# One stage for the first block's input: layer loads, latent rows, MLA attention, with 30 half-tile projections between its steps

## What is computed

```
proj = h @ w_in                                  # 1024 -> 448 + 1920 columns
c_q, c_kv, k_pe, rw = split(proj, [256, 128, 64, 1920])
# MLA attention, 4 heads
q  = rms_norm(c_q)  @ w_uq                       # per head 128 plain + 64 rotated
kv = rms_norm(c_kv) @ w_ukv                      # per head 128 keys + 128 values
s  = (q_nope @ k_nope.T + rope(q_pe) @ rope(k_pe).T) * scale
y_att = rms_norm(softmax(s) @ v)
# the delta rule's input: a centred shift along the tokens
u = rw + mu_prev * (prev(rw) - rw) + mu_next * (next(rw) - rw)
y_rwkv = delta_rule(u)                           # forwards and backwards
h = layer_norm(a*h + concat(y_att, y_rwkv) @ w_out)
h = layer_norm(a*h + mixture_of_experts(h))
```

## Time and profile before

| | us |
|---|---|
| median of 3 runs | 4491.08 (4488.44 to 4493.14) |
| the profiled execution: its own time | 4497.94 |
| its span, first to last instruction | 4496.1 |
| TensorE busy | 3495.4 (78%) |
| VectorE busy | 1609.8 (36%) |
| ScalarE busy | 790.2 (18%) |
| mean granted TensorE clock, share of full | 0.893 |

### The profile page before, as it was taken

One profiled execution on the slowest core, in us unless ns is written; L12 is line 12 of the kernel. 1 busy time (PEld: TensorE's weight loads), 2 busy tenths in 40 slices (PEclk: granted clock), 3 DMA queues, 4 the chain that ended last, 5 costly groups with the idle time before them and its releaser, 6 DMA issues. The chain is left out here.

```text
span 4496.1 us, 75562 instructions
## 1 busy us (share of the span) xinstructions
PE 3495.4 (78%) x32128; PEld 2357.7 (52%) x32128; DVE 1609.8 (36%) x2740; ACT 790.2 (18%) x1609; POOL 332.3 (7%) x462
## 2 busy tenths in 40 slices
PE   0689589774875689679773875695998899999998
PEld 0564478753443564479753443253665764444444
DVE  3144455432112244355432112316555652124421
ACT  0102222202221102222202221201334310010000
POOL 0000022001111000022001111000002200000000
PEclk9989689986897889689986897797999999999999
DMA  3200000012995200000012995700001011222221
GB/s 140 83 29 1 21 4 4 4 38 95 379 404 191 81 29 1 21 3 5 4 38 84 384 400 201 271 31 32 29 20 48 1 65 61 81 75 75 69 64 45
DMA packets 190344, 405.62 MB, mean 90 GB/s; under 512 B 39981, under 2 KB 139693, under 8 KB 161693
## 3 DMA queue, kind: packets, MB, share of 16 engines
q1 hardware_dynamic: 170029, 354.56, 21.8%
q0 software_dynamic: 9776, 29.92, 2.1%
q10 hardware_dynamic: 10240, 16.79, 1.1%
HBM read 384.45 MB, written 37.99 MB: 94 GB/s over the span
## 5 line engine op out<-in xcount | busy, mean ns | idle before, releaser
L209 PE MATMUL ps<-h,win 128*128 128x264 f32 x1216 | 275.3, 390 | 76.5 <-DMA win<-in_w_in 76.5
L2827 PE MATMUL ps<-h_lat,wt 128*128 128x512 f32 x704 | 304.7, 596 | 5.9 <-ACT h_lat L2884 5.9
L209 PEld LDWEIGHTS ps<-h,win 128*128 128x128 f32 x1216 | 233.8, 192 | 117.8 <-DMA win<-in_w_in 77.2
L1575 PE MATMUL ps<-e_w,e_xt 128*64 128x256 f32 x2048 | 248.7, 397 | 12.9 <-DMA e_w<-in_moe_w 8.6
L1575 PEld LDWEIGHTS ps<-e_w,e_xt 128*64 128x64 f32 x2048 | 175.9, 145 | 118.3 <-issue 73.1
L2827 PEld LDWEIGHTS ps<-h_lat,wt 128*128 128x128 f32 x704 | 134.6, 191 | 176.0 <-issue 174.5
L1594 PE MATMUL ps<-e_w,e_hid_t 128*64 128x512 f32 x512 | 158.1, 745 | 29.3 <-ACT e_hid_t L1622 29.3
L2784 PE MATMUL ps<-h_lat,wt 128*128 128x512 f32 x384 | 169.6, 600 | 9.6 <-DMA wt<-in_w_in 9.6
L1641 DVE TENSOR_TENSOR e_hid<-ps,e_silu 64x256 f32<-64x256 f32 x64 | 38.9, 608 | 336.2 <-ACT e_silu L1616 336.2
L2845 PE MATMUL ps<-ff_up,wt 128*128 128x512 f32 x352 | 152.2, 592 | 0.0
L1052 PE MATMUL ps<-inv,nt 48*48 48x48 f32 x3520 | 128.6, 206 | 7.0 <-issue 5.7
(11 more groups left out here) (522 smaller groups left out, 6524.9 us busy)
## 6 DMA issues: line engine op xcount, KB each, us to landing
e_w<-in_moe_w SPq DMA_DIRECT2D x192, 1024.0 KB, 9.5
wmod<-in_w_mod SPq DMA_DIRECT2D x24, 1024.0 KB, 12.8
wt<-in_w_up SPq DMA_DIRECT2D x22, 1024.0 KB, 5.1
y_rows<-e_y ACTq DMA_DIRECT2D x128, 128.0 KB, 7.4
win<-in_w_in SPq DMA_DIRECT2D x10, 1536.0 KB, 6.6
wt<-in_w_in SPq DMA_DIRECT2D x12, 1024.0 KB, 7.7
wt<-in_w_down SPq DMA_DIRECT2D x16, 704.0 KB, 4.8
wout<-in_w_out SPq DMA_DIRECT2D x8, 1024.0 KB, 5.1
```

The source lines that it names most:

```text
L209: last = pe.matmul(ps[0:rows, bank + off, 0:cols], lhsT=lhsT, rhs=rhs, start=(n == 0), stop=(n == len(pairs) - 1))
L1575: last = pe.matmul(ps[half, 2 + z, 0:EH], lhsT=xt[z][:, f, :], rhs=w[:, f, :], start=(f == 0), stop=(f == KD - 1))
L2827: last = pe.matmul(o, lhsT=w[:, i, m % 2 * P:(m % 2 + 1) * P], rhs=hl[:, i, :], start=(i == 0), stop=(i == KD - 1))
```

## The change

`load_layer_params`, `project_in`, `attention` and `mla` go. `mix_in` takes their place as one stage with 29 semaphores, followed by `mla_out` and `att_chain` as before. `first_block` calls `mix_in` and then `rwkv`. In the new stage:

- SyncE starts the latent strip of `w_in` first, then the vectors, the first `u` strip, `w_uq`, `w_ukv` and the delta rule's small matrices; the later four strips (384 columns each) start when their buffer is free.
- TensorE makes the 4 latent tiles; ScalarE evacuates them. The 15 `u` tiles are made as 30 halves of 8 matmuls, `fill(x)`, all in PSUM's bank 7, so each waits until VectorE has copied the one before to `pad` (`empty(x)`). After a second half VectorE does the three shift operations.
- Two halves stand before the sums of squares, two behind them, two behind the query, rotation, key and value tiles (`slots`, three pairs of banks in turn; ScalarE evacuates the keys and values), and one in each of the 24 attention units, between the scores of unit u+2 and the transposes of unit u.
- The probabilities have three buffers, were two. The values are weighed after every three units (half a head) in bank 6, were whole heads in banks 6 and 7. One ScalarE operation copies a unit's transposes, were two.
- All `rouse` matmuls of these stages are gone. (`rwkv` keeps its own.)

The diff, cut to its core:

```diff
-def load_layer_params(k, a, li):
...
-def project_in(k, a, li, ring, pad):
...
-def attention(k, name, units, groups, rows, pw, pt, small, masked=None, bursts=0):
...
-def mla(k, a):
...
+def mix_in(k, a, li):
+    U, HALVES, EARLY, PER = H_A * NC1, 2 * UT, 6, 3
...
+        slots = ([("q", m) for m in (4, 5, 0, 1, 2, 3)] + [("r", n) for n in range(3)]
+                 + [("k", m) for m in range(H_A)] + [("v", j) for j in range(NC1)])
...
+            @block.sync
+            def _(sp):
+                sp.dma_start(ring[0][:, :, 0:MLA_COLS], w[:, :, 0:MLA_COLS]).then_inc(win_mla, 16)
+                sp.dma_start(ring[0][:, :, MLA_COLS:512], w[:, :, MLA_COLS - ROPE:MLA_COLS]).then_inc(win_mla, 16)
...
+                strip(0)
...
+                for s in range(1, UT // PER):
+                    if s == 1:
+                        sp.wait_ge(lat_made, 4)
+                    else:
+                        sp.wait_ge(filled, 2 * PER * (s - 1))
+                    strip(s)
+                sp.wait_ge(rest_in, 48)
...
             @block.tensor
             def _(pe):
-                rouse(k, pe, 2)
+                pe.wait_ge(win_mla, 32)
...
+                def fill(x):
+                    m, h = x // 2, x % 2
+                    s, o = m // PER, m % PER * P
+                    pe.wait_ge(win_in[s % 2], 16 * (s // 2 + 1))
+                    if x:
+                        pe.wait_ge(emptied, x)
+                    else:
+                        pe.wait_ge(lat_kept, 4)
+                    for i in range(KD):
+                        last = pe.matmul(ps[:, 7, 0:HT], lhsT=ring[(s + 1) % 2][:, i, o:o + P],
+                                         rhs=k.h[:, i, h * HT:(h + 1) * HT], start=(i == 0), stop=(i == KD - 1))
+                    last.then_inc(filled, 1)
...
+                fill(0)
+                fill(1)
+                sums(0, (0, 1))
+                sums(2, (2,))
+                fill(2)
+                fill(3)
+                pe.wait_ge(uq_in, 16 * 5)
+                for t, (kind, m) in enumerate(slots):
...
+                    if kind == "r":
+                        pe.wait_ge(dve_emptied, (1, 2, 6)[m])
+                    if t >= 3:
+                        eng, n = emptied_upto(t - 3)
+                        pe.wait_ge(act_emptied if eng else dve_emptied, n)
...
+                fill(4)
+                fill(5)
...
+                score(0)
+                score(1)
+                for u in range(U):
+                    if u + 2 < U:
+                        score(u + 2)
+                    fill(EARLY + u)
+                    pe.wait_ge(normed, u + 1)
+                    if u:
+                        pe.wait_ge(kept, u)
+                    for n in range(NC1):
+                        last = pe.transpose(ps[0:TC, 4 + n // 3, (n % 3) * TC:(n % 3 + 1) * TC],
+                                            pw[:, u % 3, n * TC:(n + 1) * TC], k.ident[0:TC, 0:TC])
+                    last.then_inc(turned, 1)
+                    if u and u % 3 == 0:
+                        weigh_values(u // 3 - 1)
+                weigh_values(U // 3 - 1)
...
+                def empty(x):
+                    m, h = x // 2, x % 2
+                    dve.wait_ge(filled, x + 1)
+                    dve.tensor_copy(pad[:, 1 + h * HT:1 + (h + 1) * HT], ps[:, 7, 0:HT]).then_inc(emptied, 1)
+                    if h:
+                        u = k.u[:, m, :]
+                        dve.wait_ge(emptied, x + 1)
+                        chain(dve.tensor_scalar(u, pad[:, 1:T + 1], k.keep[:, m:m + 1], None, ALU.mult))
+                        chain(dve.scalar_tensor_tensor(u, pad[:, 0:T], k.p1("mu_prev", m), u, ALU.mult, ALU.add))
+                        chain(dve.scalar_tensor_tensor(u, pad[:, 2:T + 2], k.p1("mu_next", m), u, ALU.mult, ALU.add))
+                empty(0)
+                for n in range(2):
+                    dve.wait_ge(root, n + 1)
+                    chain(dve.reciprocal(st[:, n, :], st[:, n, :]))
...
+                    empty(n + 1)
...
@@ -3037,19 +3091,10 @@
...
-                    load_layer_params(k, a, li)
...
-                        project_in(k, a, li, ring, pad)
-                    mla(k, a)
+                mix_in(k, a, li)
                 rwkv(k, a, li)
```

More of the change, by code:

```diff
@@ new lines, in sums @@
+                def sums(bank, tiles):
+                    pe.wait_ge(squared, tiles[-1] + 1)
+                    for h in range(2):
+                        for n in tiles:
+                            last = pe.matmul(ps[:, bank + h, 0:HT], lhsT=k.ones[:, :],
+                                             rhs=sq[:, n, h * HT:(h + 1) * HT], start=(n == tiles[0]),
+                                             stop=(n == tiles[-1]))
+                    last.then_inc(summed, 1)
+                fill(0)
@@ new lines, in _, with score @@
+                fill(4)
+                fill(5)
+                pe.wait_ge(dve_emptied, sum(not x for x in by_act))
+                pe.wait_ge(act_emptied, sum(by_act))
+                def score(i):
+                    h, j = i // NC1, i % NC1
+                    b, tok = ROPE * (h % 2), slice(j * TC, (j + 1) * TC)
+                    if i >= 2:
+                        pe.wait_ge(weighed, i - 1)
+                    for half in range(2):
+                        hs = slice(half * HT, (half + 1) * HT)
+                        o = ps[0:TC, 2 * (i % 2) + half, 0:HT]
+                        pe.matmul(o, lhsT=q[:, h, tok], rhs=kn[:, h, hs], start=True, stop=False)
+                        last = pe.matmul(o, lhsT=q[b:b + ROPE, 4 + h // 2, tok], rhs=lat[b:b + ROPE, 3, hs],
+                                         start=False, stop=True)
+                    last.then_inc(scored, 1)
@@ new lines, in store @@
+                def store(x):
+                    h, half = x // 2, x % 2
+                    dve.wait_ge(valued, x + 1)
+                    dve.tensor_copy(k.att[:, h, half * HT:(half + 1) * HT], ps[:, 6, 0:HT]).then_inc(stored, 1)
+                peak(0)
+                peak(1)
+                norm(0)
+                for u in range(U):
+                    if u + 2 < U:
+                        peak(u + 2)
+                    if u + 1 < U:
+                        norm(u + 1)
+                    empty(EARLY + u)
+                    if u and u % 3 == 0:
+                        store(u // 3 - 1)
@@ L747, in mla @@
+                store(U // 3 - 1)
+        out_sq = sb("att_sq", [P, H_A, T])
+        rms_scale(k, "mla_out", [[k.att[:, h, :]] for h in range(H_A)], VD, k.ones[:, :], "rms", out_sq, q)
         with k.stage("att_chain") as (block, steps):
```

365 lines of the change are left out of this document (168 added, 197 removed).

## The result

| | before | after |
|---|---|---|
| median, same measurement, four runs each | 4491.85 (4488.44 to 4493.14) | 4382.61 (4363.92 to 4386.83) |
| the profiled execution: its own time | 4497.94 | 4363.92 |
| its span | 4496.1 | 4362.1 |
| first load to last stored head, layer 0 | 330.0 | 278.3 |
| the same, layer 1 | 330.7 | 280.2 |

The ratio is 0.975, interval 0.9721 to 0.9779: 109 us gained where 82 were forecast. The profiled execution of the changed kernel was the quickest of its four runs (the other three took 4381 to 4387), so the 134.0 us between the two profiled executions are more than the change is worth.

A forecast was written before the change was run, and what follows sets the result against it. TensorE bounds the kernel, its 251.3 us of stage work staying; only waits and half clock go. Stage 330.3 to 288.4, less 1 for its end: 40.9 a layer, 81.8 in two; 4416.1, less 6.9 gives 4409 us, range 4380 to 4448.

The forecast's parts named there:

- step 4: Around the norms: `fill(2)` waits 5.4 us for VectorE, then runs at half clock, 7.1; `fill(3)` 5.3, ending at 68.9.
- step 5: Queries, rotation, keys, values: end at 94.3 us at full clock; a clock fall at the keys adds 8, bounds 0 and 12.
- 6, two scores done: Before the attention loop: `fill(4)` and `fill(5)` with 0.7 us between, then two scores, done at 106.8 us.
- 8, last store ends: Attention's tail: transposes copied 1.2 us, last weighing 2.8, store 0.7, ending at 280.4; the old half-clock tail goes.
- Step 1 to 3: Stage start: first latent pass after 8.2 us, four latent tiles evacuated at 39.9, two halves and sums done at 50.4.
- rival B: Clock holds through key and value tiles, 8 us a layer: 4393; also over the 5.4 us idle: 4388; chance 0.22.
- Step 7: Attention loop: scores, half tiles, transposes and weighings take 168.9 us, TensorE's waits costed at nothing, ending at 275.7.
- Rival C: In the attention loop, each change of matmul kind costs 0.19 us, 14 us a layer: 4437; chance 0.18.
- Rival D: The attention loop runs at half clock, adding 2 x 168.9 us: 4747, slower than before; chance 0.04.
- rival E: In the attention units, waits on bank 7 and VectorE's order cost 1 us each, 24 a layer: 4457; chance 0.06.
- The stage's end: From last store to next stage: clearing 29 semaphores instead of ten costs 1 us more, between 0 and 2.1.

The follow-up runs named there:

- third measurement: The changed kernel unedited, run again on the same chip as a run of the kernel before: 4370.84 us, ratio 0.9753.
- 58 semaphores: The changed kernel with 29 more semaphores in the new stage, unused and only cleared at its end: 4385.96 us in one run.
- the repeat: The changed kernel measured again with no edit: 4370.9 us, ratio 0.9771 to the kernel before on the same chip.
- the third chip: Chip with one profile each of the kernel before, 4478.49 us in its run, and the unedited changed kernel, 4370.84 us, ratio 0.9753.
- the last two orders: Changed kernel with VectorE emptying halves earlier and `fill(4)` between rotation and keys: 4359.27 us; the same with all halves ahead of the attention: 4354.67 us.

## Why the prediction was right and wrong

The prediction was right in sign and mechanism: TensorE's waits and half clock in the stage go, and nothing else pays. Two terms were too large, both of the clock: its return in step 4 and, most of all, its fall in step 5. So the forecast was 26 us too slow at its centre. The measured 4382.61 lies near the low end of its range, and the ratio of 0.975, on the 4491.08 from which the forecast started, gives 4379, just below it. By its steps, from the stage's first load in layer 0:

| step | forecast | measured |
|---|---|---|
| 2, latents evacuated | 39.9 | 39.0 |
| 3, sums end | 50.4 | 50.0 |
| 4, `fill(2)` starts | 55.8 | 55.4 |
| 4, queries start | 68.9 | 65.8 |
| 5, values end | 94.3, and 8 for the clock | 91.1 |
| 6, two scores done | 106.8, and 8 | 103.9 |
| 7, length of the loop | 168.9 | 170.1 |
| 8, last store ends | 280.4, and 8 | 278.3 |

- **Step 1 to 3** hold within a microsecond. The loads need the 8.1 us to the first pass although eleven are behind, and the run with the old order shows what the new one is worth, some 9 us a layer.
- **Step 4** had the wait right (5.31 for 5.4) and oversized its price: the clock came back sooner, so that `fill(2)` took 5.61 and not 7.1, `fill(3)` 3.80 and not 5.3. That is 3 us a layer, 6 in all. In the stretch table the clock reads 0.51 from 187 to 194 and no longer.
- **Step 5 is the step that failed.** "I take it that it falls here too" cost 8 us a layer, 16 of the 27. The gap of 1.30 us at the old attention's end was taken as the model for gaps of 0.60, 0.98 and 0.97 here, and the clock held through all of them: rival B was true in the first profile after. In the change measured again the fall came in one of two layers, in the third measurement in neither, with 58 semaphores in one, so the mechanism was there, but not in every execution. The Trainium skill (TensorE: Matmul & The Clock Gate, section "Why this matters for your kernels") asks only that long idle gaps be avoided. By that rule the sum is rival B's, which came nearer, but the traces do not bear the rule out: the clock falls behind a gap of 0.97 us too. What failed most is the size. Where the fall came in the unchanged kernel it cost 1.6 us, and with the slowed rotation 1.6 and 2.8. The 8 us were worked out as if all of the values and part of a half tile would run at half clock; in fact the values behind the slow keys took their 5.31 us in the repeat, as in the first profile, and the clock read 1.00 there.
- **Step 7** held: a unit is 6.48 us where 6.42 were forecast, and TensorE idles 0.16 us of 168. Rival C (a price for each change of kind) asked for 14 us a layer; at most 1.2 show. Rival D (the loop at half clock) and rival E (longer waits) have nothing for them: clock 1.00. Of the cycling through banks that the Trainium skill (same page, section "A second HAM failure mode: psum-queue depth-cycling") describes, the new loop shows nothing either: its clock stays at 1.00.
- **The stage's end** was forecast as 1 more, and is 1.05. The 58 semaphores show that it is the clearing, and that it goes by their number.
- **The sum** had no term for stages outside, and the two profiled executions differ there by 30 us net, which by the third chip need not be of the change. The median that counts against a forecast carries less of it. 109 less 82 is 27. The two stages gained 18 more than forecast: step 5 is 16 and step 4 is 6, less some 4 that the loop and layer 1, which is 1.9 us longer than layer 0, give back. The other 9 lie outside the stages or in the scatter between executions.
- **The range's low end,** 4380, took in B, its extra and a little more. The medians of the change in three measurements are 4383, 4371 and 4371. Where the kernel before itself moves by 17 us between chips, the low end should have had that much more room.

Left open: what decides between two executions of one kernel whether the clock falls at the last keys. A hint: `fill(2)`, in which the clock comes back from its earlier fall, differs in length with it. Six profiles have the same order of steps up to the keys (the change three times, 58 semaphores, the old loads, the half tiles first), twelve layers in all. In the eight in which the keys held, `fill(2)` took 5.61 to 5.86 us; in the four in which they fell, 6.14 to 6.37. So the moment at which the clock came back may set the moment at which it can fall; no run here varied it alone. Filling the gap, as the last two orders do, makes the question go away. Open, too, is whether the stretch behind the experts is shorter because of the change, and whether the slower start of the delta rule's stage is.

## What to carry to other kernels

When work is said to be hidden under another stage, look first whether the bounding engine has room there. Here it had none, and the same stage with that work in front is as fast; what paid was that TensorE waits less from the first load to the last store: one stage in place of six (as the rows tell it, not a run of its own), the load that is waited for issued first (9 us a layer), and the next independent piece of TensorE's work set exactly where VectorE's chain would leave it waiting (some 12 us a layer more, which the change itself had left). And when a clock fall is forecast from one gap elsewhere in the trace, price it from zero up: the work that follows decides how long it lasts.

## What the runs showed of the hardware that was not expected

- The granted clock did not follow the length of a gap alone. With gaps of 0.60, 0.98 and 0.97 us and TensorE busy 7.45 of 10 us it held in one execution and fell in another of the same kernel; behind 2.82 and 3.20 us it was at 0.50 from 222 to 232.
- It came back fast: `fill(2)`, 16 passes, took 5.61 us after 5.31 idle, and the next 16 3.80; at the keys it was back within 4 us. The values' weighing at the old attention's end was busy for 10.93 us and stayed at half to its end.
- Every semaphore of a stage costs 0.055 us at its end, so 29 instead of ten cost 1.05.
- With equal durations of single matmuls (218 ns) and the same granted clock (0.98 over the delta rule of layer 0 in the three profiles of the kernel before and in the change's on the third chip), one line of the delta rule spans 245 to 249 us on two chips and 253 to 257 on another, whatever the kernel. Differences of a kernel are only to be read against the kernel before on the same chip.
- The copy of half a tile (264 columns) out of PSUM takes VectorE 0.43 us, that of a whole one 0.71. To halve the tile gives back only 40%.
